# A gated linear attention stage whose instruction order is rewritten on three engines

## The reference

```
proj = h @ w_in                          # 1024 x 3088
q, k, v, g, gk_lr = split(proj)          # 512, 512, 1024, 1024, 16 columns
log_a = log_sigmoid(gk_lr @ w_gk2 + b_gk) / 16
b = cumsum(log_a)                        # per head and channel, along the tokens
o[t] = sum over s <= t of  (sum_k q[t,k] exp(b[t,k] - b[s,k]) k[s,k]) * v[s]
o = rmsnorm(o) * silu(g)                 # 4 heads; 128 channels of q and k, 256 of v
y = o @ w_out                            # 1024 x 1024
```

## Time and profile before

| | |
|---|---|
| median of 3 runs | 1630.73 us (1629.49 to 1633.32) |
| the profiled execution: its own time | 1631.25 us |
| its span in the trace | 1629.5 us |
| PE busy over the span | 1446.8 us (89%) |
| DVE, ACT busy | 887.0 us (54%), 625.0 us (38%) |
| share of the chain that ended last: PE, DMA, SP's queue, DVE, ACT | 71%, 11%, 9%, 4%, 3% |
| mean granted TensorE clock | 0.955 |
| experts (1180 us to 1600 us of the span) | about 417 GB/s from memory |

### The profile page before, as it was taken

One profiled execution on the slowest core, in us unless ns is written; L12 is line 12 of the kernel. 1 busy time (PEld: TensorE's weight loads), 2 busy tenths in 40 slices (PEclk: granted clock), 3 DMA queues, 4 the chain that ended last, 5 costly groups with the idle time before them and its releaser, 6 DMA issues.

```text
span 1629.5 us, 23767 instructions
## 1 busy us (share of the span) xinstructions
PE 1446.8 (89%) x9182; PEld 1132.1 (69%) x9182; DVE 887.0 (54%) x1196; ACT 625.0 (38%) x832; POOL 32.8 (2%) x69
## 2 busy tenths in 40 slices
PE   7999988899999999999999999899787766767666
PEld 5888877788888888887788888777644434424433
DVE  4777666657776777766557776677621121121121
ACT  5444554454444634366654444664211011011010
POOL 4000000000000000000010000000000000000000
PEclk9999998999999999999999999999799989888989
DMA  7655542346565465644346656455999999999997
GB/s 216 207 197 189 197 139 87 104 144 208 180 201 184 156 208 179 206 155 155 129 146 202 203 176 206 154 172 192 375 398 417 418 417 419 417 418 418 418 418 310
DMA packets 170769, 396.63 MB, mean 243 GB/s; under 512 B 9507, under 2 KB 107891, under 8 KB 154336
## 3 DMA queue, kind: packets, MB, share of 16 engines
q1 hardware_dynamic: 169152, 392.20, 65.5%
q0 software_dynamic: 1440, 3.72, 1.0%
q10 hardware_dynamic: 128, 0.03, 0.0%
HBM read 393.83 MB, written 1.05 MB: 242 GB/s over the span
## 4 chain that ended last, share of the span: by engine, by line
PE 71%; DMA 11%; SPq 9%; DVE 4%; ACT 3%; issue 2%; DVEq 0%; ACTq 0%
PE psum L518 16%; PE psum L257 12%; PE psum L258 11%; PE psum L259 11%; DMA pair_ring<-in_w_exp_up 11%; PE psum L524 8%; SPq L2200 8%; PE psum L2252 4%; PE psum L2277 2%; PE psum L2296 1%; DVE low L252 1%; PE psum L981 1%; DVE hT L422 1%; ACT high L248 1%; PE psum L1386 1%
## 5 line engine op out<-in xcount | busy, mean ns | idle before, releaser
L252 DVE TENSOR_TENSOR low<-raw,high 128x2048 fp32r<-128x2048 f32 x179 | 409.6, 2291 | 190.5 <-ACT high L248 190.0
L248 ACT ACTIVATE high<-raw 128x2048 fp32r<-128x2048 f32 x179 | 341.4, 1911 | 121.7 <-PE psum L524 89.7
L518 PE MATMUL psum<-hT,high 128*128 128x512 f32 x1152 | 288.8, 393 | 2.0 <-DVE low L252 2.0
L518 PEld LDWEIGHTS psum<-hT,high 128*128 128x128 f32 x1152 | 209.8, 189 | 41.3 <-DVE low L252 2.3
L257 PE MATMUL psum<-high,hT 128*128 128x512 f32 x496 | 204.2, 412 | 11.6 <-DVE low L2536 5.0
L258 PE MATMUL psum<-low,hT 128*128 128x512 f32 x496 | 197.9, 399 | 0.0
L259 PE MATMUL psum<-high,hT 128*128 128x512 f32 x496 | 197.5, 398 | 0.0
L2277 PE MATMUL psum<-pair_ring,scratch 128*32 128x256 f32 x1984 | 135.7, 423 | 54.6 <-DMA pair_ring<-in_w_exp_up 54.5
L524 PEld LDWEIGHTS psum<-hT,low 128*128 128x128 f32 x1152 | 158.0, 191 | 11.3
L524 PE MATMUL psum<-hT,low 128*128 128x256 f32 x1152 | 161.4, 283 | 0.0
L2277 PEld LDWEIGHTS psum<-pair_ring,scratch 128*32 128x32 f32 x1984 | 65.9, 119 | 121.8 <-DMA pair_ring<-in_w_exp_up 67.5
(11 more groups left out here) (337 smaller groups left out, 1495.7 us busy)
## 6 DMA issues: line engine op xcount, KB each, us to landing
pair_ring<-in_w_exp_down SPq DMA_DIRECT2D x64, 1024.0 KB, 22.4
pair_ring<-in_w_exp_gate SPq DMA_DIRECT2D x62, 1024.0 KB, 22.1
pair_ring<-in_w_exp_up SPq DMA_DIRECT2D x62, 1024.0 KB, 22.8
raw<-in_ffn_w_gate SPq DMA_DIRECT2D x88, 512.0 KB, 4.0
raw<-in_ffn_w_up SPq DMA_DIRECT2D x88, 512.0 KB, 5.0
raw<-in_ffn_w_down SPq DMA_DIRECT2D x88, 512.0 KB, 4.3
raw<-in_gla_w_in SPq DMA_DIRECT2D x24, 512.0 KB, 4.5
raw<-in_sb_w_in SPq DMA_DIRECT2D x24, 512.0 KB, 4.7
```

Of the source, the lines that this page charges most:

```text
L248: act.activation(high[:, p % RING, :], raw_of(p), ACT.Copy).then_inc(rounded, 1)
L252: dve.tensor_tensor(low[:, p % RING, :], raw_of(p), high[:, p % RING, :].bitcast(F32), ALU.subtract).then_inc(split, 1)
L518: pe.matmul(to.rearrange("p (o n) -> p o n", o=2), w_high, both_parts, start=kk == 0, stop=False, skip_group_check=True)
```

## The change

The order on all three engines is written anew. The arithmetic stays the same but for one thing: the two memsets that cleared the scaled-k buffers go (the columns that they cleared only reach scores that `keep` does not copy).

On PE `logits` goes ahead of both halves of k. The steps go behind quarters 8, 9, 10, 11, 12, 13, 14, 16 and 17 in place of 9, 10, 11, 12, 14, 15, 17, 18 and 20, `outs` behind 20 and 21 in place of 21 and 22, and the first transpose of tile 0 behind quarter 22, ahead of the stage's last quarter. That quarter's tile 1 sum moves from bank 0 to bank 7, the banks of the transposes change, and `products(0, 1)` waits for the copy of chunk 5's tile 0, whose bank 2 it writes. ACT and DVE have their pieces, copies and level work in a new order that fits.

```
-        G_H_BANK = [[7, 3], [4, 5]]
+        G_H_BANK = [[3, 5], [4, 6]]
-        STEP_AT = {9: 0, 10: 1, 11: 2, 12: 3, 14: 4, 15: 5, 17: 6, 18: 7, 20: 8}
+        STEP_AT = {8: 0, 9: 1, 10: 2, 11: 3, 12: 4, 13: 5, 14: 6, 16: 7, 17: 8}
...
+        def in_bank(at):
+            return banks(7 if at == 2 * IN_CHUNKS - 3 else at % 3)
...  PE
             rank()
-            k_piece(0)
             turn_q()
             logits()
-            k_piece(1)
+            for half in range(2):
+                k_piece(half)
...
-                    elif at in (21, 22):
-                        outs(at - 21)
+                    elif at in (20, 21):
+                        outs(at - 20)
+                    elif at == 22:
+                        turn_half(0, 0)
...
             def front(products):
-                for tt in range(TT):
-                    turn_half(tt, 0)
+                turn_half(1, 0)
                 pe.wait_ge(turn_low, 4 * GLA_TURN + 1)
                 products(0, 0)
                 pe.wait_ge(turn_low, 4 * GLA_TURN + 2)
+                pe.wait_ge(in_copied[0], IN_CHUNKS - 1)
                 products(0, 1)
```

More of the change, by code:

```diff
@@ L1008, in quarter @@
                     kk, tok = 4 * half + k, slice(tt * P, (tt + 1) * P)
-                    ins = product(pe, banks(at % 3), hT_high[:, kk, tok], hT_low[:, kk, tok], four_k(high, q)[:, k, :],
+                    ins = product(pe, in_bank(at), hT_high[:, kk, tok], hT_low[:, kk, tok], four_k(high, q)[:, k, :],
                                   four_k(low, q)[:, k, :], start=kk == 0, stop=kk == KD - 1)
@@ L1014, in quarter, with turn_half @@
                     ins.then_inc(in_first, 1)
+            def turn_half(tt, j):
+                pe.wait_ge(h_ready, H_AT["gla"] + 2 * j + tt + 1)
+                dst = banks(G_H_BANK[j][tt])
+                for i in range(4):
+                    ins = pe.transpose(dst[:, i * P:(i + 1) * P], h[:, tt, (4 * j + i) * P:(4 * j + i + 1) * P], ident[:, :])
+                ins.then_inc(turned, 1)
             pe.wait_ge(consts, 2)
@@ L1028, in gla_pe @@
                         scores(STEP_AT[at])
-                    elif at in (21, 22):
-                        outs(at - 21)
-            def turn_half(tt, j):
-                pe.wait_ge(h_ready, H_AT["gla"] + 2 * j + tt + 1)
-                dst = banks(G_H_BANK[j][tt])
-                for i in range(4):
-                    ins = pe.transpose(dst[:, i * P:(i + 1) * P], h[:, tt, (4 * j + i) * P:(4 * j + i + 1) * P], ident[:, :])
-                ins.then_inc(turned, 1)
+                    elif at in (20, 21):
+                        outs(at - 20)
+                    elif at == 22:
+                        turn_half(0, 0)
             def front(products):
-                for tt in range(TT):
-                    turn_half(tt, 0)
+                turn_half(1, 0)
                 pe.wait_ge(turn_low, 4 * GLA_TURN + 1)
@@ L1064, in copied @@
                     act.wait_ge(used, b + 2 * n + 2)
-                act.activation(proj[:, tt, columns("gla_in", n)], banks((2 * m + tt) % 3), func,
+                act.activation(proj[:, tt, columns("gla_in", n)], in_bank(2 * m + tt), func,
                                scale=rstd[:, tt:tt + 1]).then_inc(in_copied[tt], 1)
-            def both_copied(n):
-                for tt in range(TT):
-                    copied(n, tt, ACT.Copy)
             def log_part():
@@ L1115, in gla_act @@
             piece(3)
-            both_copied(0)
+            for tt in range(TT):
+                copied(0, tt, ACT.Copy)
             piece(4)
+            turned_q()
             log_part()
-            turned_q()
             piece(5)
@@ L1123, in gla_act @@
             decays(1)
-            both_copied(2)
+            decays(2)
             piece(7)
             cross_scores()
-            decays(2)
+            decays(3)
+            copied(2, 0, ACT.Copy)
+            decays(4)
+            copied(2, 1, ACT.Copy)
             piece(8)
-            decays(3)
-            both_copied(3)
+            decays(5)
+            decays(6)
             piece(9)
-            decays(4)
-            decays(5)
+            decays(7)
+            copied(3, 0, ACT.Copy)
+            copied(3, 1, ACT.Copy)
             piece(10)
[L1135 to L1139, removed]
             for tt in range(TT):
@@ L1142, in gla_act @@
                 act.activation(v, v, ACT.Silu).then_inc(g["silu"], 1)
-            piece(13)
[L1144 to L1150, removed]
+            piece(11)
+            for tt in range(TT):
+                copied(4, tt, ACT.Copy)
+            piece(12)
+            out_squares(0)
+            out_roots(0)
+            piece(13)
+            out_squares(1)
+            out_roots(1)
+            high_half(0, 0)
+            copied(5, 0, ACT.Silu)
+            high_half(1, 0)
+            copied(5, 1, ACT.Silu)
             piece(14)
@@ L1178, in summed_logs @@
                 step(dve.tensor_tensor(glogsig, glogsig, glog, ALU.subtract))
-                for i in range(2):
-                    dve.memset(gks[i], 0.0)
                 for hd in range(GLA_HEADS):
@@ L1255, in gla_dve @@
             summed_logs()
-            piece(5)
             diff(0)
             diff(1)
+            piece(5)
             turned_k()
@@ L1267, in gla_dve @@
             diff(3)
+            scaled(2)
             piece(7)
-            scaled(2)
             diff(4)
             keep(2)
-            piece(8)
             scaled(3)
@@ L1277, in gla_dve @@
             diff(6)
+            piece(8)
             keep(4)
-            piece(9)
             scaled(5)
@@ L1282, in gla_dve @@
             keep(5)
-            piece(10)
             scaled(6)
+            piece(9)
             keep(6)
             scaled(7)
+            piece(10)
             keep(7)
-            piece(11)
-            keep(8)
-            piece(12)
             gains = gla_gain[:, :].rearrange("p (o n) -> p o n", o=1).to_broadcast([P, 2, GLA_V])
@@ L1296, in gla_dve @@
             step(ins)
[L1297 to L1303, removed]
+            keep(8)
+            piece(11)
+            piece(12)
+            inverse(0)
+            for hd in range(2):
+                ins = normed(0, hd, proj[:, 0, 2048 + hd * GLA_V:2048 + (hd + 1) * GLA_V])
+            ins.then_inc(h_ready, 1)
+            for hd in range(2, GLA_HEADS):
+                normed(0, hd, gla_gain[:, :])
+            piece(13)
+            inverse(1)
+            for hd in range(2):
+                ins = normed(1, hd, proj[:, 1, 2048 + hd * GLA_V:2048 + (hd + 1) * GLA_V])
+            ins.then_inc(h_ready, 1)
+            low_half(0, 0)
+            for hd in range(2, GLA_HEADS):
+                ins = normed(1, hd, gla_gain[:, :])
             step(ins)
-            piece(13)
-            for tt in range(TT):
-                low_half(tt, 0)
+            low_half(1, 0)
             for tt in range(TT):
```

## The result

The changed kernel took 1603.51 us in the median of 4 runs (1602.25 to 1604.39), the kernel before 1631.26 us beside it (1629.49 to 1633.32): ratio 0.9824, 95% interval [0.9808, 0.984]. Forecast were 1603.7 us, 27.0 us less; measured are 27.8 us less. The profiled execution of the changed kernel took 1602.25 us, 29.0 us less than that of the kernel before.

The account below looks back on a forecast made before the run. PE's own list plus its waits was taken as the bound; in the GLA stage 16.8 us idle and 10.6 us slow clock make 27.4 us, less 0.4 allowed: 1630.7 - 27.0 = 1603.7 us, range 1602 to 1611.

Parts of the forecast that it names:

- The bound, and the two costs: GLA stage: PE's own list bounds it; 16.8 us idle and 10.6 us of slow clock can go.
- ceiling: GLA stage: 27.4 us less if nothing waits, the stage ending at 308.50 us against 335.92.
- the quarter: PE's list in the GLA stage: each of 16 quarters takes 2.82 us at full clock, 45.12 us together.
- 308.5 to 309 named as a sign: End of the GLA stage: the last four-way transpose ends near 308.5 to 309 us, with clock 1.00 throughout.
- The allowance of 0.4 us for hand-overs: GLA stage: 0.4 us taken off the gain because the smallest covers are 0.5 and 1.1 us; forecast 27.0 us less.
- The first step: Behind quarter 8: turned_k ends at 235.51, PE wants it at 236.06, half a microsecond spare instead of 4.4 us late.
- The steps: Steps behind quarters: every scaled is ready 1.6 to 8 us ahead of PE, so the waits of scores go.
- The rival in which ACT and DVE run a round in series: Level rounds: 8.65 us against PE's 4.55, costing 38 us against 27 won; 1641 us, chance 0.05.
- The end: From outs to the last transposes: tile 1 ready before the second transpose, and the 3.1 us wait for low_half goes.
- The added wait of `products(0,1)`: End of the stage: the copy of chunk 5's tile 0 is done at 298.8, wanted 302.0.
- The slow clock that stays: GLA stage: rival that the waits go but the clock stays slow; only 16.8 us won, 1614 us, chance 0.05.

Follow-up runs that it names:

- e8: The kernel after with the two memsets put back; stage 90.63 us (one execution).
- e6: The kernel before with only logits ahead of both halves of k and turned_q ahead of log_part; stage 110.73 us (one execution).
- e5: e1 with, on ACT alone, the copies of chunks 2, 3 and 4 moved behind decays 2, 4 and 7; 1610.73 us, stage 94.69 us (one execution).
- e9: The kernel after with the first exponential of decays(4) repeated four times more, a 2.6 us delay; stage 90.54 us (one execution).
- e11: The kernel after with the first exponential of decays(4) repeated twelve times more, a 7.9 us delay; stage 95.33 us (one execution).
- e3: The kernel before with the end part alone, outs still behind quarters 21 and 22; ratio 0.9976 (1627.21 us), stage 111.02 us.
- e2: e1 plus the new step table, earlier outs and new ACT and DVE lists up to piece 12, end as before; ratio 0.9872 (1610.25 us).
- e10: The kernel after with the first exponential of decays(4) repeated seven times more, a 4.6 us delay; stage 90.13 us (one execution).
- e4: e2 with the step table and outs of the kernel before; ratio 0.9886 (1613.63 us), stage 98.65 us.
- e7: The kernel before with only the two memsets removed; stage 113.46 us (one execution).
- e1: The kernel before with logits and turned_q early, memsets gone, first two diffs ahead of piece 5; ratio 0.9973 (1626.67 us), stage 111.13 us.

## Why the prediction was right

**How close.** 1603.7 forecast and 1603.51 measured agree to 0.2 us, which is less than the runs of one kernel differ (1602.25 to 1604.39), and partly luck. The stage lost 28.1 us and not 27.0. The kernel before measured 1631.26 us beside it, not the 1630.7 that I had started from. What is right beyond luck is the account: which waits go, that the slow clock goes with them, and that nothing behind takes it back.

**The bound, and the two costs.** Right. PE's own list at full clock was put at 89.75 us, it is 88.9. The idle 16.8 us went but for 0.16. The slow clock had cost 11.5 us, not 10.6, and so the "ceiling" of 27.4 us was too low; the stage lost 28.1. The mis-sized term is the quarter: 2.82 us holds behind a step, but where three follow each other PE takes 8.2 us for them (from 298.07, the end of the second transpose, to 306.28), 2.74 each. For the same reason, and because the stage starts 0.64 us earlier, its end is at 307.16 us and not at the 308.5 to 309 named as a sign. The allowance of 0.4 us for hand-overs wasn't needed.

**The first step.** Right in its sign and nearly in its size: cover of 0.5 us forecast, 0.7 measured. The scan came sooner than I had laid out, because the memsets had taken 2.15 us of the path (1.9 by my reading of the rows; the wait ahead of the first one belongs to them). e8 shows how thin this cover is: with the memsets back PE waits 1.3 us. But e6 shows that with the old table's position of the first step neither the memsets' removal nor the later piece 5 is needed. They pay for moving the steps up by a quarter, which itself brought almost nothing.

**The steps.** Right that no wait is left, and right in the reason that was read from the profile, ACT copying chunks ahead of the exponentials: e5 removes all level waits by that alone. The rival in which ACT and DVE run a round in series and are too slow for PE is ruled out by the kernel after, in which no step waits; e9 to e11 add how much is spare at step 5, 4.5 to 5 us, and that behind the 2.9 us wait of e11 no other follows. The prediction weighed the change as a whole and did not say which of its parts earns what; by the runs, the new step table is the part that earns least.

**The end.** Right. e3 takes 6.15 us alone: 3.1 us of waiting and 3.05 us of slow clock (busy 97.31 against 100.36). On top of e2 it is 4.8 us (93.83 to 89.05), with the same 3.0 us of waiting but 1.8 us of slow clock (90.67 to 88.89): behind the wait for `low_half` the clock was low for 6.8 us in the kernel before and for 3.4 us in e2. The wait of 0.65 us is not in the difference; e3 keeps it, and in e2 the earlier `outs` had taken it. The added wait of `products(0,1)` doesn't show in the waits of the kernel after.

**The slow clock that stays.** Forecast with 0.05, and not seen: between 215 and 335 us the clock of the kernel after is 1.00. The Trainium skill, "TensorE: Matmul & The Clock Gate", section "A second HAM failure mode: psum-queue depth-cycling", tells of a clock that swings because PE idles briefly and often between groups of matmuls that cycle through banks. Nothing of the kind shows here: nine steps and sixteen quarters through eight banks ran at a clock of 1.00 in the kernel after, in e8 and in e10. But PE idled only 0.16 us in the kernel after, so the short idle moments that the page names as the cause were absent; the runs neither bear it out nor speak against it. That e9 lost the clock once is another thing, at another place, with no cycling of banks near it.

## What to carry to other kernels

When a busy engine waits again and again for a chain over two others, look in their lists for an instruction that itself waits for the busy engine and stands ahead of a link of the chain: that closes a loop, and moving it behind the link (here the copies of three chunks) is worth more than a new timetable. Price a wait on TensorE with the slow clock behind it: here 16.8 us of waiting had brought 11.5 us more, very unevenly from wait to wait. And lay the other engines' work beside the bound engine's times before rewriting: where the cover comes out at half a microsecond, it is real, but it is spent by the next small thing put in its way.

## What the runs showed of the hardware that I had not expected

**The clock falls without a wait.** In e4, e6, e9 and e11 the granted clock is at its lower level for 3.4 us, starting at 220.9 to 222.1 us, about 1 us behind the end of the logits; in the other seven kernels with the logits first it is 1.00 there, and so it is in the three that have the old order (before, e3, e7). PE had not waited longer than 0.16 us. What it did before the fall is, in the new order, a row of light work with no break but those 0.16 us: the rank product (24 matmuls on 16-column weights), four matmuls for the rows, eight transposes of q, and the logits on 16 rows; in the old order the first half of k lies between the first part and the last. That this row of light work is the cause is argued from where the fall lies, not shown: no run moved it. It can't be all of the cause, as seven kernels have the row and no fall. The kernel after, e9, e10 and e11 have the same lists up to there, and two of the four fall, so it differs from execution to execution and not from kernel to kernel. The four with the fall are those whose stage starts earliest in the trace, at 217.30 to 217.89 us, where the other seven start at 218.00 to 218.56; e7, in the old order, starts at 217.13 without a fall. Whether the moment at which the row comes decides, or what made those executions earlier, stays open. The fall costs 1.5 us (busy 90.38 in e9 against 88.89). A part of k between the rank rows and the logits would be the thing to try.

**The price of a wait varies.** The same 4.9 us wait had 6.8 us at the lower level in it and behind it in the kernel before and in e3, and 10.2 us in e1, e6 and e7. The same wait of 1.56 us had 3.4 us in the kernel before, e3 and e6, and 6.8 us in e1 and e7. Waits of 2.2 us at the last of the three late steps had none in any kernel, nor had the 1.32 us of e8 or the 2.3 us for `turned_k` of e7; 2.9 us in e11 had 3.4 us. At most half of such a length is lost, as part of it can lie in the wait itself. So a single execution can't tell what a wait of 1 to 3 us costs, and stage lengths of kernels with waits, taken from one execution each, can differ by 1.7 us or 3.4 us for this alone.
